# Row and layer norms by halves: mean spread and taken off apart, factors spread without a diagonal, other orders at four joints

## The chip, the cores and the metric

One core of a Trainium2 chip. The time is microseconds of one execution on the device; the median of several runs counts. TensorE (PE) does the matrix products into PSUM, VectorE (DVE) and ScalarE (ACT) the elementwise work, GpSimd (POOL) a few additions, SyncE (SP) issues the loads of the weights.

## The reference, cut to what matters

A transformer block and two hybrid layers over 512 tokens of 1024 channels, all in float32. The first block (with 16 meta tokens beside the 512):

```
h  = h + rms_norm(mix @ w_out, ln_post_mix)       # mix: two attentions, sliding and forgetting
hn = rms_norm(h, ln_pre_ffn)
ff = (silu(hn @ gate) * (hn @ up)) @ w_down
h  = h + rms_norm(ff, ln_post_ffn)
```

Each of the two layers that follow:

```
u    = x * (1 + scale) + shift                     # scale, shift, gate from c, by one matrix
proj = u @ w_in                                    # convolution, short convolution, latent attention, gates
m    = g_a * y_a + g_b * y_b + g_c * y_c
x    = layer_norm(alpha * x + gate * (m @ w_o), ln_g, ln_b)
```

rms_norm divides by sqrt(mean(x^2) + 1e-6) over a token's 1024 channels; layer_norm takes off the mean first and divides by sqrt(var + 1e-5).

## The kernel before, in words

**Layout.** Activations lie transposed: 128 partitions are 128 channels, 8 tiles (KD) hold the 1024 channels, and the free axis is the 512 tokens, in some places in two halves c = 0, 1 of 256 (HC). A norm therefore sums over partitions and over the 8 tiles.

**Weights.** 134 slots of 1 MB (128 x 2048) stream through three buffers. SP loads slot g when slot g - 3 is used up (slot_done). ACT copies the slot to `w_hi` in a rounded format (`slot_hi`, L1330), and DVE subtracts to get `w_lo` (`slot_lo`, L1887); both can go by quarters (`part`). A product is three matmuls, hi x hi, hi x lo, lo x hi (`mm3`, L631 to L633), and so each moving operand has a high and a low half too (`Xh` by ACT, `Xl` by DVE, `x_rest` L2196).

**Order.** Each engine has one queue, written out by hand in program order. Semaphores join them: a product waits for `x_lo`, a square by ACT for the tile's read by DVE and for the last use of its buffer (there are two, `sq`), an addition to `acc` for its square.

**A norm.** ACT squares, DVE or POOL add the squares into `acc`, PE sums over partitions with a matmul against a column of ones, tokens on the partitions (`token_sums` L672, `down_sums` L1059, `block_sums` L1089). ACT takes the root, DVE the reciprocal `ri`, one value per token. To bring it back along the free axis, DVE multiplies the identity by `ri` (four blocks of 128 x 128, or two for a half: L1938, L2228, L2538), and PE multiplies a matrix of ones with that diagonal (`spread` L687, `down_spread` L1073, `half_spread` L1121): each partition of a PSUM bank then holds the factor of each token.

**The joints.** These are the places that the change touches.
- Start: norm 0 of the first block.
- First border: the last two slots of w_out (slots 11 and 12, tiles n = 0 to 7 read by DVE at L2100), the post-mix norm, the pre-FFN input, then the first two gate/up slots, S_GU and S_GU + 1 (`two_slots` L974). Ahead and between PE runs filler, `keep_busy` (L635), matmuls with no use of their result. DVE splits S_GU behind tile 2 and S_GU + 1 behind tile 5; ACT copies the latter behind square 4.
- Second border: the last w_down slot by halves (`down_slot` L1022), the post-FFN norm of half 0 while half 1 is multiplied, `down_x` (L2231: multiply, add to h), the two ACT copies of the next input (L1597), `x_rest`, and the first two slots of layer 0, whose products wait for x_lo tile by tile (L1142 to L1163). `second_half` (L2214) reads half 1's tiles; its tiles 2 to 7 count `late_y`, of which the first layer's products want four (L1141).
- Third border: the same between layer 0 and layer 1, with a layer norm. `half_mean` (L2541) makes delta (the mean), its diagonal, and the variance from the mean of squares; `half_root` the factor's diagonal; `half_spread` spreads both into one bank, and `half_x` (L2559) subtracts the mean and then multiplies, tile by tile. The sums of half 0 stand among the products of half 1, tile 0 (`SUM_STEPS`, L1304), those of half 1 at step 3 of the next layer (L1145).
- Tail: the same behind layer 1, where no products follow; ACT applies gain and offset and SP stores.

## Time and profile before

| | us |
|---|---|
| median of 3 runs (lowest, highest) | 1720.53 (1719.82, 1721.81) |
| profiled execution, its own time | 1722.89 |
| its span, first to last instruction | 1720.9 |
| PE busy | 1692.8 (98%) |
| DVE, ACT, POOL busy | 1074.5, 726.1, 155.0 |
| PE waiting for `Xl` of a product | 6.2 |

The mean granted clock of PE is 0.992 of full speed. The span counts from the first to the last instruction; the execution's own time has some 2 us around it. In the timelines each row has start, duration, engine, line of the kernel, operation, output <- inputs, shape, count, and in brackets the idle time of the engine just before it with what ended it. The ends of matmuls are modelled, and matmuls overlap: the spacing of starts is the better measure of their cost.

### The profile page before, as it was taken

Reading aid. Unit: us, or ns where it says so; the run is one execution under the profiler, and the core shown is the slowest. Engines: PE = TensorE matmul, PEld = TensorE weight load, DVE = VectorE, ACT = ScalarE, POOL = GpSimd, SP = SyncE. Lnnn points to the kernel's source line nnn. Section 1 sums busy time; section 2 is a strip of 40 time slices with the busy share of each in tenths; the row PEclk is TensorE's granted clock in tenths of the full one; section 3 lists DMA queues with packets and bytes.
Section 4 is the critical chain, followed back from the end, with each engine's and each line's share of the span. In section 5 each row is a group of like instructions: output and inputs, shape, how many; then the busy total and the mean of one; then the engine's idle time right before and its main releaser. Section 6 shows DMA issues by size and latency. Waiting matters only on the chain.

```text
span 1720.9 us, 21479 instructions
## 1 busy us (share of the span) xinstructions
PE 1692.8 (98%) x8592; PEld 1404.2 (82%) x8592; DVE 1074.5 (62%) x1811; ACT 726.1 (42%) x1155; POOL 155.0 (9%) x144
## 2 busy tenths in 40 slices
PE   8999999999999999999999999999999999999997
PEld 8877777888888888888888888889888888888886
DVE  7455556866665437735869665667654769666465
ACT  4436563322222237576423222536566433232533
POOL 2100000000000000111100000021211100000012
PEclk9999999999999999999999999999999999999998
DMA  4321012555554321321222222221322122222221
GB/s 177 129 98 50 26 50 86 190 198 194 192 193 168 111 93 57 117 79 74 74 89 93 95 93 97 96 98 50 123 98 75 53 95 98 98 98 98 82 90 50
DMA packets 31138, 177.49 MB, mean 103 GB/s; under 512 B 3677, under 2 KB 5869, under 8 KB 13886
## 3 DMA queue, kind: packets, MB, share of 16 engines
q1 hardware_dynamic: 22048, 144.71, 23.3%
q0 software_dynamic: 8608, 31.21, 5.1%
q8 instruction: 68, 1.11, 0.3%
q10 hardware_dynamic: 382, 0.19, 0.0%
q14 instruction: 32, 0.26, 0.0%
HBM read 171.28 MB, written 4.78 MB: 102 GB/s over the span
## 4 chain that ended last, share of the span: by engine, by line
PE 81%; DVE 2%; issue 1%; DMA 0%; ACT 0%; DVEq 0%; ACTq 0%
PE ps L631 26%; PE ps L632 25%; PE ps L633 25%; PE ps L1247 1%; PE ps L1235 1%; DVE h L1872 1%; PE ps L1091 1%; PE ps L669 0%; DMA w_raw<-in_w 0%; DVE w_lo L1872 0%; PE ps L1224 0%; ACT w_hi L1320 0%; PE ps L1126 0%; DVE acc L1872 0%; DVE tmp L1879 0%
## 5 line engine op out<-in xcount | busy, mean ns | idle before, releaser
L631 PE MATMUL ps<-Xh,w_hi 128*128 128x512 f32 (+2 forms) x1760 | 666.2, 379 | 8.1 <-DVE Xl L1872 6.2
L633 PE MATMUL ps<-Xh,w_lo 128*128 128x512 f32 (+2 forms) x1760 | 655.1, 372 | 0.0
L632 PE MATMUL ps<-Xl,w_hi 128*128 128x512 f32 (+2 forms) x1760 | 655.0, 372 | 0.0
L1872 DVE TENSOR_TENSOR w_lo<-w_raw,w_hi 128x2048 fp32r<-128x2048 f32 (+1 forms) x161 | 312.2, 1941 | 252.8 <-ACT w_hi L1320 252.5
L631 PEld LDWEIGHTS ps<-Xh,w_hi 128*128 128x128 f32 x1760 | 331.2, 188 | 72.9 <-issue 11.4
L1320 ACT ACTIVATE w_hi<-w_raw 128x2048 fp32r<-128x2048 f32 (+1 forms) x158 | 260.5, 1652 | 293.0 <-DMA w_raw<-in_w 270.3
L632 PEld LDWEIGHTS ps<-Xl,w_hi 128*128 128x128 f32 x1760 | 331.3, 188 | 58.7 <-issue 2.6
L633 PEld LDWEIGHTS ps<-Xh,w_lo 128*128 128x128 f32 x1760 | 331.0, 188 | 58.3
L1879 DVE SCALAR_TENSOR_TENSOR cacc<-ain,vec,cacc 128x512 f32<-128x512 f32 x240 | 166.4, 765 | 0.0
L1320 ACT ACTIVATE gt<-ps 128x512 f32<-128x512 f32 x48 | 28.6, 597 | 200.6 <-PE ps L633 200.5
L631 PE MATMUL ps<-act_h,w_hi 128*128 128x512 f32 (+1 forms) x192 | 71.5, 372 | 0.6 <-DVE act_l L1872 0.6
L632 PE MATMUL ps<-act_l,w_hi 128*128 128x512 f32 (+1 forms) x192 | 71.3, 371 | 0.0
L633 PE MATMUL ps<-act_h,w_lo 128*128 128x512 f32 (+1 forms) x192 | 71.3, 371 | 0.0
L1320 ACT ACTIVATE Pc<-ps,nmax 128x128 f32<-128x128 f32 (+1 forms) x64 | 33.9, 529 | 79.3 <-DVE nmax L2344 79.1
L1320 ACT ACT_TABLE_LOAD x46 | 59.0, 1283 | 3.8 <-issue 3.0
L2145 DVE CUSTOM_DVE_ANT_0 ada_prod<-ada_w,cact 128x1024 f32<-128x1024 f32 x44 | 53.8, 1223 | 0.1
L583 POOL DMA_DIRECT2D ada_w<-in_w_ada x48 | 25.5, 531 | 276.3 <-DVE ada_sum L2145 276.3
L631 PEld LDWEIGHTS ps<-act_h,w_hi 128*128 128x128 f32 x192 | 36.2, 188 | 7.2 <-DVE w_lo L1872 1.0
L633 PEld LDWEIGHTS ps<-act_h,w_lo 128*128 128x128 f32 x192 | 36.1, 188 | 6.3
L632 PEld LDWEIGHTS ps<-act_l,w_hi 128*128 128x128 f32 x192 | 36.2, 188 | 6.2
L607 POOL TENSOR_TENSOR Ql<-Q,Qh 128x512 fp32r<-128x512 f32 x16 | 20.8, 1303 | 218.9 <-ACT Kh L1320 218.9
L1872 DVE TENSOR_TENSOR tmp<-ps,R 128x512 f32<-128x512 f32 x22 | 15.2, 690 | 34.3 <-PE ps L633 33.2
(322 smaller groups left out, 2186.2 us busy)
## 6 DMA issues: line engine op xcount, KB each, us to landing
w_raw<-in_w SPq DMA_DIRECT2D x134, 1024.0 KB, 4.8
ada_w<-in_w_ada POOLq DMA_DIRECT2D x48, 512.0 KB, 4.6
bias_scratch<-brow POOLq DMA_DIRECT2D x2, 1312.0 KB, 5.9
h<-in_xT SPq DMA_DIRECT2D x4, 512.0 KB, 5.9
out<-h SPq DMA_DIRECT2D x8, 256.0 KB, 2.1
bias<-bias_scratch POOLq DMA_DIRECT2D x1, 1024.0 KB, 8.8
bias<-bias_scratch POOLq DMA_DIRECT2D x1, 512.0 KB, 4.6
cact<-in_c POOLq DMA_DIRECT2D x1, 512.0 KB, 6.3
```

The source lines that it names most:

```text
L583: pool.dma_start(ada_w[:, t % 2, :], a["w_ada"][t, :, :]).then_inc(adaw_in[t % 2], 16)
L607: nc.gpsimd.tensor_tensor(Ql[:, :], Q[:, hd, :], Qh[:, :], ALU.subtract)
L631: nc.tensor.matmul(o_, whi, xhi, start=start, stop=False)
L632: nc.tensor.matmul(o_, whi, xlo, start=False, stop=False)
L633: return nc.tensor.matmul(o_, wlo, xhi, start=False, stop=stop)
L1091: last = nc.tensor.matmul(bank(b, 1, c0=t), src[:, HC * c + t * P:HC * c + (t + 1) * P], ones[:, 0:1], start=start and t == 0, stop=stop a ...
L1235: last = nc.tensor.transpose(bank(2 + b, P, c0=P * k), Pc[:, P * (tri(b) + k):P * (tri(b) + k + 1)], ident[:, :])
L1247: last = nc.tensor.matmul(bank(B_O, P, DH * e, DH * (e + 1), c0=P * b), Vc[:, k, DH * (hd - 1 + e):DH * (hd + e)], PTc[e][:, P * (tri(b) + ...
L1320: return nc.scalar.activation(o_, i_, f, **kw)
L1872: return nc.vector.tensor_tensor(o_, a_, b_, op)
L1879: return nc.vector.scalar_tensor_tensor(o_, a_, s_, b_, op0, op1)
L2145: nc.vector.tensor_tensor_reduce(prod, ada_w[:, par, :], cact[:, :], 1.0, 0.0, ALU.mult, ALU.add, ada_sum[:, par:par + 1]).then_inc(ada_do ...
```

## The change

- All spreads: no diagonal is made. The stationary operand of the spread is the column `ri[:, t]` itself, repeated over 128 columns, and the moving one is the identity. `diag_done` becomes `factor_done`, set by the reciprocal.
- First border: `keep_busy(2)` ahead of the sums goes. DVE splits S_GU behind tile 4 and S_GU + 1 behind the whole loop, ACT copies S_GU + 1 behind square 6, and DVE adds squares 5 and 6 between the reads of tiles 6 and 7.
- Second border: `x_rest` is taken out of `down_x` as `down_rest` and comes one or two steps later; quarters 0 and 1 of the slot are copied and split earlier; `down_x` of half 0 is mixed with the reads and additions of half 1; the spread of half 0 goes before tile 4 of the last slot, the sums and spread of half 1 before steps 5 and 6.
- Third border and tail: mean and factor are spread by matmuls of their own, into banks of their own; `half_sub` subtracts the mean as soon as it is spread, while variance, root and reciprocal are made, and `half_x` only multiplies. The sums have another order (mean first, then acc, then the two squares). In the tail four of the six sums of half 1 stand among the last tile's products.

```diff
-SUM_STEPS = (1, 2, 4, 5, 6, 7)
+SUM_ORDER = (0, 1, 2, 5, 3, 4)
...
             def spread(n, b):
-                pe.wait_ge(diag_done, n)
+                pe.wait_ge(factor_done, n)
                 for t in range(NB):
-                    last = nc.tensor.matmul(bank(b, P, c0=P * t), ones[:, :], tmp[:, 1, t * P:(t + 1) * P],
+                    last = nc.tensor.matmul(bank(b, P, c0=P * t), ri[:, t:t + 1].to_broadcast([P, P]), ident[:, :],
                                             start=True, stop=True)
...
-            keep_busy(2, bank(B_O), T)
             token_sums(1, 2 * KD - 1, (KD - 1,), B_ST)
...
                                 if j == 3:
                                     down_sums(0, 0)
-                                if j == 5:
+                                if j == 4:
                                     down_spread(0, 0)
...
-                    block_sums(var_bank, acc, c, False, True).then_inc(sum_full, 1)
+                    block_sums(var_bank, acc, c, True)
...
+            def block_spread(b, col, c):
+                for t in range(2):
+                    last = nc.tensor.matmul(bank(b, P, c0=P * t), col[:, 2 * c + t:2 * c + t + 1].to_broadcast([P, P]),
+                                            ident[:, :], start=True, stop=True)
+                return last
+            def mean_spread(L, c):
+                pe.wait_ge(delta_done, 2 * L + c + 1)
+                block_spread(spread_banks(L, c)[0], delta, c).then_inc(m_spread, 1)
+            def factor_spread(L, c):
+                pe.wait_ge(factor_done, SPREADS1 + 2 * L + c + 1)
+                block_spread(spread_banks(L, c)[1], ri, c).then_inc(r_spread, 1)
...
-                        if c == 0 and k == 3:
+                        if c == 0 and k == 4 and L:
+                            mean_spread(L - 1, 1)
+                        if c == 0 and k == (3 if L else 5):
...
-                        if c == 0 and k == KD - 3:
+                        if c == 0 and k == (5 if L else 6):
...
-                            if c == 1 and j == 0 and k in SUM_STEPS:
-                                half_sum(L, 0, SUM_STEPS.index(k))
-                            if c == 1 and j == 1 and k == 4:
-                                half_spread(L, 0)
+                            if c == 1 and j == 0:
+                                if k == 4:
+                                    mean_spread(L, 0)
+                                if k < len(SUM_ORDER):
+                                    half_sum(L, 0, SUM_ORDER[k])
+                            if c == 1 and j == 1 and k == 1:
+                                factor_spread(L, 0)
+                            if L + 1 == LAYERS and c == 1 and j == 1 and k >= 4:
+                                half_sum(L, 1, (0, 5, 1, 3)[k - 4])
...
                 if L + 1 == LAYERS:
-                    half_sums(L, 1)
-                    half_spread(L, 1)
+                    half_sum(L, 1, 2)
+                    half_sum(L, 1, 4)
+                    mean_spread(L, 1)
+                    factor_spread(L, 1)
...
                     if n == 2:
                         slot_hi(S_GU)
-                    if n == 4:
+                    if n == 6:
                         slot_hi(S_GU + 1)
...
-                    if n > 1:
+                    if n == 4:
+                        slot_lo(S_GU)
+                    if 1 < n < 6:
                         add_y_square(n - 1)
-                    if n == 2:
-                        slot_lo(S_GU)
-                    if n == 5:
-                        slot_lo(S_GU + 1)
+                    if n == 6:
+                        add_y_square(5)
+                        add_y_square(6)
+            slot_lo(S_GU + 1)
...
             down_add(1, 1)
+            slot_lo(SLOTS1 + 1, 0)
             down_roots(0)
             second_half(3)
-            slot_lo(SLOTS1 + 1, 0)
+            slot_lo(SLOTS1 + 1, 1)
             down_x(0, 0)
+            down_x(1, 0)
+            second_half(4)
+            down_rest(0, 0)
             down_add(2, 1)
-            second_half(4)
+            down_x(2, 0)
+            down_rest(1, 0)
             second_half(5)
...
+                def half_sub(j, c):
+                    cs = slice(HC * c, HC * (c + 1))
+                    if j == 0:
+                        ve.wait_ge(m_spread, 2 * L + c + 1)
+                        ve.wait_ge(sq_ready, SQ1 + SQUARES2 * (L + 1) - 2 + 2 * c)
+                    centred[j, c] = own.mark(tt(h[:, j, cs], h[:, j, cs], bank(spread_banks(L, c)[0], HC), ALU.subtract))
...
+                half_delta(0)
+                for j in range(3):
+                    half_sub(j, 0)
+                half_var(0)
+                half_sub(3, 0)
                 half_root(0)
                 if L + 1 == LAYERS:
+                    for j in range(4, KD):
+                        half_sub(j, 0)
+                    half_tile(KD - 2, 1)
+                    for j in range(KD):
+                        half_x(j, 0)
+                    half_tile(KD - 1, 1)
+                    half_delta(1)
+                    half_sub(0, 1)
+                    half_var(1)
+                    half_sub(1, 1)
+                    half_root(1)
+                    half_sub(2, 1)
+                    for j in range(KD):
+                        half_x(j, 1)
+                        if j + 3 < KD:
+                            half_sub(j + 3, 1)
```

## Rows read from the trace of the kernel before

**Rows 1.** Whom PE waited for: us in total, times, longest.

```profile
PE ps L631 <- DVE Xl L1872: 6.2, 7, 1.6
```

**Rows 2.** Timeline of PE, first border: start, us, instruction, idle before.

```profile
274.30 1.88 PE L639 MATMUL ps<-mask,ident 128*128 128x512 f32 x4
278.84 1.86 PE L678 MATMUL ps<-ones,acc 128*128 128x1 f32 x8 [2.67 <-DVE acc L1872]
...
284.12 1.81 PE L691 MATMUL ps<-tmp,ones 128*128 128x128 f32 x8
...
289.63 0.47 PE L631 MATMUL ps<-Xh,w_hi 128*128 128x512 f32 x1 [1.12 <-DVE Xl L1879]
```

**Rows 3.** Timeline of DVE, first border.

```profile
274.10 2.29 DVE L1872 TENSOR_TENSOR w_lo<-w_raw,w_hi 128x2048 fp32r<-128x2048 f32 x1 [0.83 <-ACT w_hi L1320]
...
278.11 0.68 DVE L1872 TENSOR_TENSOR acc<-acc,sq 128x512 f32<-128x512 f32 x1
...
285.97 0.75 DVE L1879 SCALAR_TENSOR_TENSOR tmp<-y,vec,ps 128x512 f32<-128x512 f32 x1 [2.13 <-PE ps L691]
```

**Rows 4.** Timeline of ACT, first border.

```profile
272.09 1.90 ACT L1320 ACTIVATE w_hi<-w_raw 128x2048 fp32r<-128x2048 f32 x1
...
277.07 0.63 ACT L1320 ACTIVATE sq<-y 128x512 f32<-128x512 f32 x1 [2.56 <-issue]
```

**Rows 5.** Windows: length, busy PE, PEld, DVE, ACT, POOL, then granted clock, DMA, GB/s.

```profile
278.50:279.00 0.50, 0.16 (x1) 0.16 (x1) 0.29 (x1) 0.40 (x1) 0.00 (x0) 0.86 0.13 49
285.50:286.00 0.50, 0.50 (x4) 0.46 (x4) 0.03 (x1) 0.00 (x0) 0.00 (x0) 0.82 0.00 0
1705.50:1706.00 0.50, 0.50 (x5) 0.50 (x4) 0.47 (x3) 0.42 (x1) 0.00 (x0) 0.63 0.34 115
```

**Rows 6.** Timeline of PE, third norm, among products.

```profile
308.80 0.95 PE L678 MATMUL ps<-ones,acc 128*128 128x1 f32 x8
...
311.77 1.05 PE L691 MATMUL ps<-tmp,ones 128*128 128x128 f32 x8
```

**Rows 7.** Timeline of PE, second border.

```profile
654.27 0.28 PE L631 MATMUL ps<-act_h,w_hi 128*128 128x256 f32 x1
...
654.63 0.28 PE L631 MATMUL ps<-act_h,w_hi 128*128 128x256 f32 x1
...
656.32 0.35 PE L631 MATMUL ps<-Xh,w_hi 128*128 128x256 f32 x1 [1.17 <-DVE Xl L1872]
...
662.62 0.39 PE L631 MATMUL ps<-Xh,w_hi 128*128 128x256 f32 x1 [1.59 <-DVE Xl L1872]
```

**Rows 8.** Timeline of DVE, second border.

```profile
653.04 0.48 DVE L1879 SCALAR_TENSOR_TENSOR tmp<-y,vec,ps 128x256 f32<-128x256 f32 x1
653.56 0.43 DVE L1872 TENSOR_TENSOR h<-h,tmp 128x256 f32<-128x256 f32 x1
653.90 0.42 DVE L1872 TENSOR_TENSOR acc<-acc,sq 128x256 f32<-128x256 f32 x1
```

**Rows 9.** Timeline of PE, third border.

```profile
1178.90 0.28 PE L631 MATMUL ps<-Xh,w_hi 128*128 128x256 f32 x1
...
1180.78 0.35 PE L631 MATMUL ps<-Xh,w_hi 128*128 128x256 f32 x1 [1.36 <-DVE Xl L1872]
...
1182.81 0.39 PE L631 MATMUL ps<-Xh,w_hi 128*128 128x256 f32 x1 [0.37 <-DVE Xl L1872]
```

**Rows 10.** Timeline of PE, tail.

```profile
1703.86 0.58 PE L1091 MATMUL ps<-ones,R 128*128 128x1 f32 x4 [0.82 <-DVE h L1879]
...
1709.20 2.08 PE L1126 MATMUL ps<-tmp,ones 128*128 128x128 f32 x8 [1.70 <-DVE tmp L1876]
```

**Rows 11.** Timelines of DVE and of ACT, tail.

```profile
1711.31 6.39 DVE L1872 TENSOR_TENSOR h<-h,ps 128x256 f32<-128x256 f32 x16 [0.60 <-PE ps L1126]
...
1717.73 0.60 ACT L1320 ACTIVATE h<-h,vec 128x256 f32<-128x256 f32 x1 [0.19 <-DVE h L1872]
```

**Rows 12.** Timeline of PE, start.

```profile
15.40 2.08 PE L691 MATMUL ps<-tmp,ones 128*128 128x128 f32 x8 [0.42 <-DVE tmp L1876]
```

More of the change, by code:

```diff
@@ L385, in program, with sum_banks, spread_banks @@
         B_O, B_ST = 6, 7
+        def sum_banks(L, c):
+            return (3, 4) if c == 0 else (0, 1) if L + 1 < LAYERS else (2, 5)
+        def spread_banks(L, c):
+            return (B_O, B_ST) if c == 0 else (0, 1) if L + 1 < LAYERS else (3, 4)
         LAT_BANK = (2, 3, 4, 5, 0, 6)
@@ L1073, in down_spread @@
             def down_spread(c, b):
-                pe.wait_ge(diag_done, 4 + c)
+                pe.wait_ge(factor_done, 4 + c)
                 for t in range(2):
-                    last = nc.tensor.matmul(bank(b, P, c0=P * t), ones[:, :], tmp[:, 1, HC * c + t * P:HC * c + (t + 1) * P],
-                                            start=True, stop=True)
+                    last = nc.tensor.matmul(bank(b, P, c0=P * t), ri[:, 2 * c + t:2 * c + t + 1].to_broadcast([P, P]),
+                                            ident[:, :], start=True, stop=True)
                 last.then_inc(r_spread, 1)
@@ L1609, in _ @@
             tf.add(KD - 1)
+            for part in range(2):
+                slot_hi(SLOTS1 + 1, part)
             for j in range(3):
@@ L1612, in _ @@
             down_root(0, 0)
-            slot_hi(SLOTS1 + 1, 0)
             down_square(3, 1)
             down_x(0, 0)
+            down_x(1, 0)
             down_square(4, 1)
-            slot_hi(SLOTS1 + 1, 1)
-            down_x(1, 0)
-            for j in range(5, KD):
-                down_square(j, 1)
+            down_x(2, 0)
+            down_square(5, 1)
+            down_x(3, 0)
             slot_hi(SLOTS1 + 1, 2)
-            down_x(2, 0)
-            down_x(3, 0)
+            down_square(6, 1)
+            down_x(4, 0)
+            down_x(5, 0)
+            down_square(7, 1)
             slot_hi(SLOTS1 + 1, 3)
-            down_x(4, 0)
             down_root(1, 1)
-            for j in range(5, KD):
+            for j in range(6, KD):
                 down_x(j, 0)
@@ L1935, in token_roots @@
                 ve.wait_ge(rt_done, norm + 1)
-                own.link(nc.vector.reciprocal(ri[:, :], rs[:, :]))
-                for t in range(NB):
-                    last = ts(tmp[:, 1, t * P:(t + 1) * P], ident[:, :], ri[:, t:t + 1], None, ALU.mult)
-                last.then_inc(diag_done, 1)
+                nc.vector.reciprocal(ri[:, :], rs[:, :]).then_inc(factor_done, 1)
             for j in range(1, KD):
@@ L2225, in down_roots @@
                 ve.wait_ge(rt_done, 4 + c)
-                own.link(nc.vector.reciprocal(ri[:, two], rs[:, two]))
-                for t in range(2 * c, 2 * c + 2):
-                    last = ts(tmp[:, 1, t * P:(t + 1) * P], ident[:, :], ri[:, t:t + 1], None, ALU.mult)
-                last.then_inc(diag_done, 1)
+                nc.vector.reciprocal(ri[:, two], rs[:, two]).then_inc(factor_done, 1)
             def down_x(j, c):
@@ L2595, in _ @@
-                for j in range(KD):
-                    half_x(j, 1)
-                if L + 1 == LAYERS:
+                half_delta(0)
[3 more added lines that the diff above has]
+                half_sub(3, 0)
+                half_root(0)
+                if L + 1 == LAYERS:
+                    for j in range(4, KD):
[14 more added lines that the diff above has]
+                            half_sub(j + 3, 1)
@@ L2598, in _ @@
                     ve.wait_ge(ln_out, 2 * KD)
                     return
-                x_rest(2 * KD * (L + 2) - 1, KD - 1, slice(HC, T))
+                half_sub(4, 0)
+                second_slot(0)
+                half_x(0, 0)
+                half_sub(5, 0)
+                half_x(1, 0)
+                second_slot(1)
+                half_rest(0, 0)
+                half_sub(6, 0)
+                half_x(2, 0)
+                half_tile(KD - 2, 1)
+                half_rest(1, 0)
+                half_sub(7, 0)
@@ new lines, in _ @@
+                half_x(3, 0)
+                half_tile(KD - 1, 1)
+                half_rest(2, 0)
+                second_slot(2)
+                half_x(4, 0)
+                half_rest(3, 0)
+                half_x(5, 0)
+                second_slot(3)
+                half_rest(4, 0)
+                half_x(6, 0)
+                half_rest(5, 0)
+                half_x(7, 0)
+                half_delta(1)
+                half_rest(6, 0)
+                half_var(1)
+                half_rest(7, 0)
@@ L2601, in _ @@
+                half_root(1)
+                half_sub(0, 1)
+                half_sub(1, 1)
+                half_x(0, 1)
+                half_sub(2, 1)
+                for j in range(1, KD):
+                    half_x(j, 1)
+                    if j + 2 < KD:
+                        half_sub(j + 2, 1)
+                    half_rest(j - 1, 1)
+                half_rest(KD - 1, 1)
                 assert own.n == OWN2, own.n
```

133 lines of the change are left out of this document (61 added, 72 removed).

## The prediction

> **What bounds the kernel now.** The page comes first: TensorE (PE) is busy for 98% of the span at a granted clock of 0.992, and every other engine has room, so time can only come out of places where PE stands still or does filler. The list of whom PE waited for shows where they are: the largest entry is products that wait for the low half of their moving operand, 6.2 us in seven waits [rows 1]. The timeline puts five of these at the second and third border; beside them stand the first border, where small sums, filler and a spread run one after the other [rows 2], and the tail, where PE has no product left and VectorE (DVE) and ScalarE (ACT) finish alone [rows 10, 11]. So the reader should see four joints between stretches of dense products, and read the change from them. The reference point is the profiled execution, 1722.89 us (span 1720.9 and 1.99 around it); it is 2.36 above the median of the runs, and I take that off at the end.
>
> **Start (norm 0).** The four scaled identity blocks go, and the spread reads the reciprocal itself. PE waited 0.42 for them [rows 12]; the filler ahead of the spread ends just where that wait began, so no more than this comes free, and the split pieces that DVE does meanwhile are shorter than the spread. Bounds 0 and 0.42; value 0.4.
>
> **First border.** Before: products are issued until 274.30, then 1.88 of filler, 2.67 of idle until the last addition to acc, sums, filler, spread; the first multiply stands at 285.97 and the first product at 289.63 [rows 2, 3]. The addition was late because DVE took up the 2.29 us split of the second gate/up slot at 274.10, ahead of the tiles 6 and 7, which it should have read [rows 3]. The change moves this split behind the loop, the first slot's split two tiles back, and ACT's half of the second slot (1.90) behind square 6.
> New order, step by step from the same end of products. A tile takes twelve products, 2.72 us, so tile 6 is complete near 271.8; reading, squaring and adding it are about 0.68 + 0.63 + 0.68 [rows 3, 4], so acc is whole near 273.8, before the products end. Hence the acc sums run at once, and only tile 7 is left: read from about 274.5 to 275.1, squared until 275.8. ACT's slot copy, begun near 273.05, ends at 274.95, by its 1.90 [rows 4], and just doesn't delay that square; were it 0.5 us later, so would be the border. Sums of square 7 at the full clock, 0.8 to 0.95 [rows 6], end near 276.7. The slot's split on DVE (2.2, from 275.1) now stands ahead of the reciprocal, which comes at 277.4; that is as late as ACT's root and PE's one remaining filler allow. Spread 1.05 [rows 6]: first multiply near 278.74 instead of 285.97, and the 3.66 us from there to the first product stay. Gain 7.2. The two filler products that are dropped are worth nothing by themselves; what they guarded is the clock, below.
>
> **Clock at this border.** By the means of half-microsecond windows the granted clock fell to 0.5 (1.2 GHz) near 278.85, after PE had stood still since 276.2, and came back near 285.7, after some 6.8 us of sums, filler and spread; sums of 8 instructions took 1.86 there, 0.95 at the full level [rows 2, 5, 6]. In the tail it fell near 1705.65, with PE issuing one-column sums since 1703.86 [rows 5, 10]. It did not fall over the stops of 1.17 to 1.59 at the second border [rows 7]. In the new order the longest stop before the products is about 0.5, then sums, 0.94 of filler and the spread, and three fillers afterwards; I take the full clock. If it falls all the same, sums, filler and spread from 275.9 on cost 0.85 + 0.94 + 1.0 more: gain 4.4 instead of 7.2.
> The Trainium skill speaks against the change here: TensorE: Matmul & The Clock Gate, section Why this matters for your kernels, asks to leave no long stops between bursts, since they bring the half rate back, and its Part 1 says that the chip's watch runs free of the kernel's start, so that the same order may fall in one run and not in another. By that rule, removing filler is a risk, and the border would give 4.4. This trace agrees with the fall at 278.85 and at 1705.65 and shows shorter stops without one.
>
> **Third norm inside the products.** Its spread at 311.77 waited for nothing; the chain from its end to the next tile is unchanged. 0.
>
> **Second border.** Three products take 0.36 us, a step of twelve 1.44 [rows 7]. Products would have gone on at 654.99; steps 0 and 2 started at 656.32 and 662.62, so that 1.33 was lost ahead of the first and 6.30 - 2.88 = 3.42 in the two that follow, in all 4.75. New queue of DVE, from 651.96, with 0.34 for a half tile's addition, 0.86 for a multiply and its addition [rows 8], about 0.60 for a quarter split (a quarter of 2.29 and an instruction's fixed part): second_half 3, quarter 1, down_x 0 and 1, second_half 4 (3.0), rest 0 (behind ACT's two copies of block 0, 655.05), add 2, down_x 2, rest 1, second_half 5 (2.2): 657.3. That last one matters, since the next layer's first product waits for the fourth late_y, which second_half 5 gives: it stood before 655 and now stands behind rest 1. So the first product comes later than before, near 657.45: a stop of 2.46. From there the low halves are ready at 656.9, 658.8, 660.7, 662.8, 664.4, each before its step (657.45 + 1.44 each); the sums, moved two steps later, find their squares; about 0.14 is lost at the last step. Gain 4.75 - 2.6 = 2.2. Bounds: 4.7 with no stop left, -0.5 if DVE is a further 2.7 late.
>
> **Third border.** PE lost 1180.78 - 1179.26 = 1.52 and 1182.81 - 1180.78 - 1.44 = 0.59 [rows 9]. The mean's sums move one or two steps earlier, and its spread and subtraction run under tile 0's products while the variance's sums and root are made; behind the factor only the multiply is left. By the same counting the delta comes 0.7 earlier, the first multiply near 1176.9, the first low half near 1178.5, ahead of the last product. ACT's quarter copy ahead of half_x 1 leaves low half 1 at 1180.05, within 0.1 of its step. The added spread costs PE 0.1. Gain 2.0; bounds 0.5 (the first stop merely halved, the second kept) and 2.1. The second half's sums at step 3 find their inputs 1.5 us early.
>
> **Tail.** Before: sums from 1703.86, spread at 1709.20, sixteen operations from 1711.31, last ACT operation 1717.73 to 1718.33 [rows 10, 11], then 2.57 of output. New: four sums go among the last tile's products, about 0.45 each (0.58 for a lone one, [rows 10]), so these end at 1704.7, not 1703.0. Then tile 7's half, 0.5; its sums and the delta, 0.8; mean spread to the first subtraction, 0.75: 1706.8. Variance, ACT's root, reciprocal and two subtractions take 1.1; the factor's spread is half of the 2.08 that eight took [rows 10]: 1708.95. Thirteen operations then remain, not sixteen, and a multiply no longer waits for its own subtraction: 0.34 apart [rows 8] instead of 6.39 / 16 = 0.40; ACT follows at 0.5 for the last two: end at 1714.3 against 1718.33. Gain 4.0; bounds 2.5 (spreads at the half clock throughout, 0.40 kept) and 4.6.
>
> **Sum.** 0.4 + 7.2 + 2.2 + 2.0 + 4.0 = 15.8: 1707.1 for a profiled execution, 1704.7 for the median. Between the joints PE runs without stops that hang on an absolute time, so I expect nothing to be given back.
>
> **Not in the trace: a stationary operand that repeats one column.** 32 matmuls, 64 loads, take `ri` or `delta` broadcast over 128 columns where `ones` or a diagonal stood; the number of loads stays. The nearest row is the spread with a dense operand, eight loads and passes in 1.05 [rows 6], and I take that. Below it a gain of 0.05 each at most is left; above, nothing in the trace bounds it, and it is a rival.
> The Trainium skill prices it, on the page TensorE: Matmul & The Clock Gate, section LDWEIGHTS, by the number of columns alone, with 107 ns for 128 columns at its rate; an estimate by that page adds nothing to the sum. No run here shows it.
>
> **Rivals.**
> - The clock falls at the first border: +2.8, 1707.5. For: two falls at such places. Against: the new stops are shorter than those it outlasted.
> - The second and third border give nothing (+4.2, 1708.9): a DVE queue of the same length, or ACT's two copies per block, keep the low halves as late as before. For: the first product of the second border is later by my own count. Against: at the third border nothing but the split of the chain is needed.
> - On the other side, one mechanism: the broadcast loads are slow. All 64 stand at joints where PE or DVE waits for them. 15.8 / 64 = 0.25 us more for each eats the gain, 0.30 makes the kernel slower by over 0.2%, 0.5 gives 1721. For: no such load in the trace. Against: the loads are many columns of one value, no more bytes than before.
>
> **How the numbers follow.** A measurement tells 0.2% (3.4 us) from no change. Forecast 0.6 (own range 1702.5 to 1706.5), clock 0.18, borders 0.13, loads 0.05 (slower), and 0.04 for several terms failing at once, most of it within the bound. The range 1702.5 to 1710 takes in the first three cases nearly whole. Faster 0.92 (the first three and a part of the last), same 0.03, slower 0.05.
>
> **What would show it.** First border: no 2.29 us split between the tile reads, acc sums right behind the last product, first multiply some 4.3 after it, clock 1.0. Second: one stop of about 2.4 before the first product and none behind steps 0 to 2. Third: no stop over 0.2. Tail: four sum groups among the last products, thirteen operations behind the last spread. A spread over 1.3 us at the full clock, or stops that stay at the second and third border, would make it wrong.

## The result and the profile after

| | before | after |
|---|---|---|
| median of the timed runs, us (lowest, highest, runs) | 1721.17 (1719.82, 1722.25, 4) | 1710.26 (1710.12, 1711.40, 4) |
| ratio after / before, 95% interval | | 0.9938 [0.9922, 0.9954] |
| profiled execution, us | 1722.89 | 1710.12 |
| its span, us | 1720.9 | 1708.3 |

The kernel is 10.9 us faster by the medians, and 12.8 in the profiled executions (12.6 of it in the span). The forecast was 15.8 and 1704.7, its range ended at 1710.0: the direction is right, the time lies 0.26 outside. Ratios and their intervals, here and below, are of undisturbed executions; two slow ones stand outside them (2119 us of the kernel before, 3373 us of one further down).

The changed kernel's page, its line of the engines, and then its list of whom PE waited for (total us, times, longest) answer to [rows 1]: of the seven waits for `Xl`, 6.2 us, one of 1.1 and two of 0.3 together are left; a wait for `y` (the first product of the second border) and one for `act_l` (w_down) have come up.

```profile
PE 1687.0 (99%) x8588; PEld 1401.2 (82%) x8588; DVE 1065.2 (62%) x1779; ACT 723.3 (42%) x1155; POOL 154.8 (9%) x144
```

```profile
PE ps L640 <- DVE y L1905: 2.1, 1, 2.1
PE ps L640 <- DVE act_l L1905: 1.7, 1, 1.7
PE ps L1130 <- DVE ri L2593: 1.2, 1, 1.2
PE ps L640 <- DVE Xl L1912: 1.1, 1, 1.1
```

The view that settles where the time went is none of the page's: both traces hold the same 7080 matmuls of `mm3` (called products from here on, as in the prediction's counts), so the start of each can be subtracted from the start of the same product before. Where this lead grows or shrinks, the change gains or loses. The entries are read to within 0.03.

| place | forecast | lead gained in the profiled pair |
|---|---|---|
| start | 0.4 | 0.53 |
| first border | 7.2 | 7.06 |
| third norm | 0 | 0.0 |
| w_down stage | 0 | -1.06 |
| second border, and 20 us behind it | 2.2 | 2.28, then -0.57 |
| third border | 2.0 | 0.84 |
| tail | 4.0 | 3.53 |
| sum | 15.8 | 12.6 |

**First border**, PE of the changed kernel, against [rows 2]: sums right behind the products, one stop of 0.71, spread 1.05 where it was 1.81. The first product stands at 282.08 where it stood at 289.63.

```profile
273.81 0.95 PE L687 MATMUL ps<-ones,acc 128*128 128x1 f32 x8
275.47 1.05 PE L692 MATMUL ps<-ones,sq 128*128 128x1 f32 x8 [0.71 <-ACT sq L1344]
276.38 1.10 PE L648 MATMUL ps<-mask,ident 128*128 128x512 f32 x2
277.32 1.05 PE L700 MATMUL ps<-ident,ri 128*128 128x128 f32 x8
278.21 2.74 PE L648 MATMUL ps<-mask,ident 128*128 128x512 f32 x6
...
282.08 0.47 PE L640 MATMUL ps<-Xh,w_hi 128*128 128x512 f32 x1 [1.13 <-DVE Xl L1912]
```

**w_down stage**, the changed kernel's chain of work that ended last (start, us, what), then PE's row: a weight slot took 7.38 us from issue to landing (median 4.8 in this stage), and the products behind it stood still for 1.67.

```profile
589.96 7.38 DMA w_raw<-in_w
597.35 0.03 ACTq L1352
597.37 0.04 issue
597.42 1.93 ACT w_hi L1344
...
599.44 2.29 DVE w_lo L1905
601.73 0.61 DVE act_l L1905
```

```profile
602.48 0.47 PE L640 MATMUL ps<-act_h,w_hi 128*128 128x512 f32 x1 [1.67 <-DVE act_l L1905]
```

**Third border**, windows of the changed kernel (length, busy PE, PEld, DVE, ACT, POOL, granted clock, DMA, GB/s). PE has no wait left, but the clock is at 0.5 for some 3.4 us, behind 24 one-column sums issued in one go from 1175.39 to 1177.98 (24 as the profile counts: each of the kernel's twelve float32 matmuls shows as two). In the profiled execution of before, none of the windows from 1165 to 1194 was under 1.00; the second fence has its window behind the sums.

```profile
1178.00:1179.50 1.50, 1.50 (x14) 1.50 (x14) 0.99 (x4) 1.12 (x3) 0.00 (x0) 0.92 0.00 0
1179.50:1181.00 1.50, 1.50 (x9) 1.50 (x9) 0.27 (x1) 0.00 (x0) 0.00 (x0) 0.50 0.00 0
1181.00:1182.50 1.50, 1.50 (x9) 1.50 (x9) 0.48 (x2) 0.00 (x0) 0.00 (x0) 0.50 0.00 0
1182.50:1184.00 1.50, 1.50 (x14) 1.50 (x14) 0.46 (x2) 0.00 (x1) 0.00 (x0) 0.94 0.00 0
```

```profile
1185.00:1190.00 5.00, 5.00 (x45) 4.88 (x44) 2.16 (x10) 1.61 (x4) 0.00 (x0) 1.00 0.00 0
```

**Second border and tail**: PE, then DVE's last group, against [rows 7, 10, 11]. One stop of 2.15 replaces three; a stop of 0.30 follows 25 us later, for a weight slot's low half; in the tail four groups of sums stand among the products (the first at 1692.39), and thirteen operations remain behind the last spread.

```profile
650.80 0.35 PE L640 MATMUL ps<-Xh,w_hi 128*128 128x256 f32 x1 [2.15 <-DVE y L1905]
...
676.30 0.50 PE L640 MATMUL ps<-Xh,w_hi 128*128 128x512 f32 x1 [0.30 <-DVE w_lo L1905]
...
1692.39 0.50 PE L1099 MATMUL ps<-ones,R 128*128 128x1 f32 x4
...
1696.34 0.61 PE L1099 MATMUL ps<-ones,h 128*128 128x1 f32 x4 [0.58 <-DVE h L1912]
1696.81 0.59 PE L1099 MATMUL ps<-ones,sq 128*128 128x1 f32 x4
...
1699.11 1.22 PE L1130 MATMUL ps<-ident,ri 128*128 128x128 f32 x4 [1.17 <-DVE ri L2593]
```

```profile
1700.38 4.40 DVE L1905 TENSOR_TENSOR h<-h,ps 128x256 f32<-128x256 f32 x13 [1.00 <-PE ps L1130]
```

### The profile page after: what moved, and what is told of

Read it like the earlier page. It is cut to its first block, busy times and chain, and to the rows that moved or that the text cites. A ratio compares the mean times of both kernels' runs of the same rounds, so it can differ in the third digit from the quotient of the medians.

```text
span 1708.3 us, 21445 instructions
## 1 busy us (share of the span) xinstructions
PE 1687.0 (99%) x8588; PEld 1401.2 (82%) x8588; DVE 1065.2 (62%) x1779; ACT 723.3 (42%) x1155; POOL 154.8 (9%) x144
## 4 chain that ended last, share of the span: by engine, by line
PE 96%; DVE 2%; DMA 1%; ACT 1%; issue 0%; ACTq 0%; DVEq 0%
PE ps L640 29%; PE ps L642 29%; PE ps L641 28%; PE ps L1264 1%; PE ps L1252 1%; PE ps L875 1%; PE ps L905 1%; PE ps L838 1%; DVE h L1905 1%; PE ps L1099 1%; PE ps L897 1%; PE ps L678 1%; PE ps L870 0%; PE ps L836 0%; DMA w_raw<-in_w 0%; PE ps L849 0%
```

## The experiments

Theory: the forecast's mechanisms hold, and what is missing went to (a) falls of TensorE's clock at joints that I had taken as safe, (b) the weight slot in w_down, (c) an order in the tail that costs instead of giving, and (d) a reference point that was no typical execution. Main rival: the missing 3 us belong to one accidental execution. Ratios are to the kernel before on the same chip; a difference of two ratios whose intervals overlap is no proof by itself, and then the products of the profiled executions are what is read. Leads are again those of single products in the profiled executions, against the changed kernel's first profile.

### Both kernels once more

The changed kernel, no edit:

> The changed kernel once more, unchanged. Theory A: its two unforeseen losses belong to the order of its instructions. Then the stop of 1.67 us of TensorE near 602 (a w_down product behind a weight slot whose transfer took 6.15 instead of 3.5 us, begun 0.3 us after a block of instructions was fetched by DMA) and the fall of the clock to 0.5 near 1179 (3.4 us long, right behind the 24 one-column sums) come again within 0.3 us of their places, and the span is 1708.3 within 1. Rival: both are accidents of one execution; then at least one is missing, the span is 1.3 to 3.2 us shorter, and the median of the timed runs is below 1709.

Ratio 0.9935 [0.9921, 0.9949], median 1710.87, profiled span 1709.9. Half of each came: the missing time is there again in sum, partly at other places. The stop in w_down came again (1.98, a transfer of 6.45 us by its packets, begun 0.25 behind a fetch of instructions), with a small one (0.23) ahead of it. The fall near 1179 did not: that border came out 1.53 better. Instead the clock fell at the second border, 1.49 worse there, and at the first, 0.45 worse. PE's row and, in the second fence, the window of the fall in this execution:

```profile
602.99 0.47 PE L640 MATMUL ps<-act_h,w_hi 128*128 128x512 f32 x1 [1.98 <-DVE act_l L1905]
```

```profile
652.50:655.50 3.00, 3.00 (x16) 3.00 (x16) 2.97 (x9) 2.85 (x6) 0.00 (x0) 0.50 0.27 112
```

The kernel before, no edit:

> The kernel before once more, unchanged, for its clock. Theory: whether the clock falls at a border varies between executions of the same kernel, so this one has other falls than the first (278.86 for 6.83 us only): at the first border half as long or none, or a new one at the second or third border; and its span differs from 1720.9 by 0.5 to 3 us, by the places where the clock fell and by the transfer in the w_down stage that the fetch of a block of instructions delays. Rival: the falls belong to the kernel; then there is one fall, at 278.9 within 0.5, and the span is 1720.9 within 0.5.

One execution, 1721.72, span 1719.7. The fall at the first border lasted half as long (the sums took 1.05 there, not 1.86 as in [rows 2]), there was one at the third border that the first profile lacked, right behind the old order's own 24 sums (1183.59 to 1186.18), and no slow transfer in w_down. So the old order falls at the third border too, in some executions. The window of this fall:

```profile
1186.50:1189.50 3.00, 3.00 (x16) 3.00 (x16) 2.90 (x11) 1.78 (x4) 0.00 (x0) 0.50 0.00 0
```

From start to the first border's end the changed kernel's lead over this execution is 6.20, against 7.55 over the first one.

### The first border alone

The old order of this border comes back (the first slot's split and the squares too); the new spread stays.

```
-                    if n == 6:
+                    if n == 4:
                         slot_hi(S_GU + 1)
...
+                    if n == 5:
+                        slot_lo(S_GU + 1)
...
-            slot_lo(S_GU + 1)
...
+            keep_busy(2, bank(B_O), T)
             token_sums(1, 2 * KD - 1, (KD - 1,), B_ST)
```

> The changed kernel with the first border's order as before: split of the second gate/up slot ahead of the reads of tiles 6 and 7, its copy on ScalarE behind square 4, two filler products ahead of the sums. Theory: this border alone gives 7.0 of the 12.6 us, so the kernel takes 7.0 (6.5 to 7.5) us more than the changed one, and the clock falls near 278 again. Rival: part of what is gained there is given back at later places that hang on other clocks (the weight slots of w_down), then it is 5 to 6.3 more.

Ratio 0.9962 [0.9949, 0.9975], median 1715.11: 4.2 above the changed kernel on the same chip, under both expectations. By products the undone border cost 5.4; the wait for acc is back (277.50, stop 2.67), but the clock's fall was half as long as in [rows 2, 5]. So of the 7.06 in the profiled pair some 1.6 was the longer fall of that one execution of before, and the changed order falls there too, in other executions. PE's rows of this execution:

```profile
277.50 1.05 PE L687 MATMUL ps<-ones,acc 128*128 128x1 f32 x8 [2.67 <-DVE acc L1906]
278.41 1.03 PE L692 MATMUL ps<-ones,sq 128*128 128x1 f32 x8
```

### Sums at the third border in two groups

```
-                        if c == 0 and k == (3 if L else 5):
-                            if L:
-                                for i in SUM_ORDER:
-                                    half_sum(L - 1, 1, i)
+                        if c == 0 and k in (2, 3) and L:
+                            for i in SUM_ORDER[3 * (k - 2):3 * (k - 1)]:
+                                half_sum(L - 1, 1, i)
...
```

> The changed kernel with the 24 one-column sums of the second half at the third border put in two groups, the mean's 12 at step 2 and the variance's 12 at step 3, with twelve products between them, instead of all at step 3. Theory: the clock falls at 1179 because 2.6 us of one-column sums stand together; split, it stays full there, and the border gains 1.2 to 1.6 us. Rival 1: the fall does not hang on their standing together, and comes again; change within 0.3. Rival 2: the mean's sums wait for their inputs at step 2 and open a stop; 0.3 to 1 slower there.

Ratio 0.9924 [0.9911, 0.9937], median 1708.48, 2.4 below the changed kernel on the same chip, with overlapping intervals. No fall and no stop at this border, which came out 1.55 better than in the first profile. One execution without a fall proves little, since the unchanged order has such executions; the test by the opposite follows.

### The first half's sums in one go

```
-                                if k == 4:
+                                if k == 6:
                                     mean_spread(L, 0)
-                                if k < len(SUM_ORDER):
-                                    half_sum(L, 0, SUM_ORDER[k])
+                                if k == 4:
+                                    for i in SUM_ORDER:
+                                        half_sum(L, 0, i)
```

> The changed kernel with the first half's 24 one-column sums, which stand in six groups among as many steps of the last tiles of each layer, all at one step, and the mean's spread two steps later; the third border stays as changed. Theory: standing together is what lets the clock fall, so that it now falls also near 1166 to 1172 (end of layer 0) or near 1686 to 1692 (end of layer 1), in at least one of the two, 1.4 to 1.6 us each, and the median is 1 to 3 us above the changed kernel's. Rival: together or apart is no matter; no fall at either place, and the same time within 0.5.

Ratio 0.9953 [0.9941, 0.9966], against 0.9935 for the changed kernel: 0.18%, 3.1 us, the upper end of what the theory gave, though the intervals overlap. The clock fell in the middle of the layer's end, where it had never fallen in the eleven other profiles of changed orders; PE's rows, then the window of this execution:

```profile
1161.34 0.50 PE L1099 MATMUL ps<-ones,R 128*128 128x1 f32 x4
1161.70 1.03 PE L1099 MATMUL ps<-ones,h 128*128 128x1 f32 x8
1162.59 0.59 PE L1099 MATMUL ps<-ones,acc 128*128 128x1 f32 x4
1163.04 1.29 PE L1099 MATMUL ps<-ones,sq 128*128 128x1 f32 x8
```

```profile
1163.70:1167.00 3.30, 3.30 (x17) 3.30 (x17) 0.24 (x1) 0.00 (x0) 0.00 (x0) 0.50 0.00 0
```

The layer's end came out 2.4 worse, 0.53 of it a stop for the factor (the edit put the mean's spread two steps later). At the end of layer 1, the other place named, it did not fall. Its third border, with the sums in one go as before, happened to stay at the full clock.

### The second border: each bank's own wait, or filler

```
-                if L == 0:
-                    pe.wait_ge(late_y, 4)
...
+                            if L == 0 and c == 0 and k == 0:
+                                pe.wait_ge(late_y, i + 1)
...
             down_rest(0, 0)
-            down_add(2, 1)
-            down_x(2, 0)
-            down_rest(1, 0)
             second_half(5)
+            down_x(2, 0)
+            down_rest(1, 0)
+            down_add(2, 1)
             down_add(3, 1)
```

> The changed kernel with another start of the products at the second border: each of the first four products waits only for its own PSUM bank to be read, and VectorE takes second_half 5 two operations earlier. The first product came at 650.80 behind a stop of 2.15. Theory: the stop ends 1.5 to 1.8 earlier (stop 0.4 to 0.7); the low halves of steps 3 to 6 are late then, and 0.3 to 1.6 of it is kept behind step 7, likeliest 0.8; with the shorter stop the clock does not fall near 652, as it did in three of five executions of such orders (1.5 us each). Rival: the low halves on VectorE are the bound from step 2 on, and the same end of the border comes out, within 0.2, with other stops; the clock then falls or not as before.

Ratio 0.9928 [0.9916, 0.9941], median 1709.50. The first product came 1.85 earlier, and all of it was lost again by step 7 (the lead over the changed kernel is 1.68 ahead of the border, 1.52 behind it): the rival is right, the low halves on DVE and ACT are the bound. No fall at this border. The stops of this execution:

```profile
647.27 0.35 PE L640 MATMUL ps<-Xh,w_hi 128*128 128x256 f32 x1 [0.30 <-issue]
651.03 0.39 PE L640 MATMUL ps<-Xh,w_hi 128*128 128x256 f32 x1 [0.60 <-DVE Xl L1905]
652.88 0.39 PE L640 MATMUL ps<-Xh,w_hi 128*128 128x256 f32 x1 [0.17 <-DVE Xl L1905]
655.00 0.38 PE L640 MATMUL ps<-Xh,w_hi 128*128 128x256 f32 x1 [0.43 <-DVE Xl L1905]
```

The other way, filler in the stop:

```
                 if L == 0:
+                    pe.wait_ge(bank_read[1], FILL1[1])
+                    keep_busy(8, bank(1), T)
                     pe.wait_ge(late_y, 4)
```

> The changed kernel with eight filler products (512 columns, 0.234 us each) in the stop of 2.15 us ahead of the second border's first product. Theory: the clock falls at this border in some executions because TensorE stands still there; with the filler it stays full, the first product comes at the same time within 0.1, and the median is 0.5 to 1.5 us shorter than the changed kernel's. Rival 1: the fall comes of something else (it began 1.2 us after the stop had ended); it is seen at 650 to 657 all the same. Rival 2: the filler delays the products by 0.2 to 0.5.

Ratio 0.9954 [0.9941, 0.9966], median 1712.64: slower than the changed kernel, by my own mistake. A filler of 512 columns takes 0.88 here, not 0.234 (a float32 product shows as two matmuls, x16 for eight), so they held the products back by 4.16:

```profile
648.89 7.03 PE L648 MATMUL ps<-mask,ident 128*128 128x512 f32 x16
```

The clock did stay full at this border; the right number of fillers, two, is in the last group below.

### The tail's sums behind the last tile

```
-                            if L + 1 == LAYERS and c == 1 and j == 1 and k >= 4:
-                                half_sum(L, 1, (0, 5, 1, 3)[k - 4])
...
-                    half_sum(L, 1, 2)
-                    half_sum(L, 1, 4)
+                    for i in (0, 5, 1, 3, 2, 4):
+                        half_sum(L, 1, i)
```

> The changed kernel with the second half's four groups of sums behind the last tile's products again, not among them; the rest of the tail stays as changed. Among the products they cost 1.26 us of TensorE time by the trace; behind them they stand on the path to the end, about 1.3 at the full clock and 2.6 at 1.2 GHz. Theory: their place is worth 0 to 0.5 if the clock is full until they end, 1 to 1.5 if it falls among them (it fell at 1696.9 to 1698.1 in two executions), so the kernel is 0.2 to 1.5 us slower. Rival: the last tile's addition on VectorE and the root hide them, and nothing changes (within 0.2), so the whole gain of the tail is in the split of mean and factor.

Ratio 0.9934 [0.9921, 0.9948], median 1709.65: not to be told from the changed kernel by the timed runs, as the rival has it. By products the tail of this execution is 0.83 shorter, where five executions with the changed tail agree with the first within 0.02 (in one more, the second run of the changed kernel, the clock fell earlier in the tail and it took 1.2 longer); in the three kernels further down with the sums behind, it is 0.59, 1.36 and 0.85 shorter. So the theory is wrong in sign. The rows show why: less the lead that this execution had before, the products end 1.77 earlier, and the sums now fill the 0.58 in which PE had waited for tile 7.

```profile
1693.37 0.50 PE L1099 MATMUL ps<-ones,R 128*128 128x1 f32 x4
...
1695.08 0.58 PE L1099 MATMUL ps<-ones,h 128*128 128x1 f32 x4
1695.52 0.58 PE L1099 MATMUL ps<-ones,sq 128*128 128x1 f32 x4
1695.97 0.69 PE L1130 MATMUL ps<-ident,rsum 128*128 128x128 f32 x4
1697.83 1.23 PE L1130 MATMUL ps<-ident,ri 128*128 128x128 f32 x4 [1.17 <-DVE ri L2591]
```

### More warm-up at the start

```
-            warm_up(8, 4)
+            warm_up(28, 4)
```

> The changed kernel with 28 instead of 8 warm-up products (128 columns, 0.127 us each) ahead of the first norm's sums, in the 2.77 us that TensorE waits there. It does two things. First, theory: the clock, at 0.5 from 11.9 to 18.7 in the changed kernel, stays full; the sums take 0.95 instead of 1.87, the spread 1.05 instead of 1.92, and the first product comes 1.5 to 1.8 us earlier, all of it kept. Rival: the clock falls there whatever TensorE does, or the first product hangs on the weights' low half; gain under 0.3. Second, all later blocks of TensorE's instructions are fetched 20 products earlier (4.7 us in the w_down stage). Theory: the stop of 1.67 near 602 comes of the fetch that lies on the transfer of a weight slot, so it goes (another 1.0 to 1.7). Rival: the transfer is late for another reason, and the stop stays at 1.4 to 1.9. Both theories together: 2.5 to 3.4 us less than the changed kernel.

Ratio 0.9936 [0.9923, 0.9948], median 1711.38: nothing gained. The twenty added products took 4.6 us, not 2.5 (the same miscount), so the sums came 1.57 late, at 13.88; they and the spread then ran at the full clock (0.95 and 1.16). The first product, at 18.81, came 0.40 earlier than in the first profile, but that is no gain: in the ten profiles with the changed kernel's own warm-up it stood between 17.93 and 19.50, early where the clock's fall at the start lasted 3.4 us and late where it lasted 6.8. In w_down the stop near 602 was gone; a stop of 0.45 stood at 558.88 instead, behind a transfer of 4.79 us.

### Together

The edits of the third border (two groups), the tail (sums behind) and the second border (own waits); then the same with two fillers in the stop instead of the own waits; then the first with `warm_up(18, 4)`.

> Three edits on the changed kernel: the 24 sums at the third border in two groups (as in e3), the tail's sums behind the last tile (as in e4), each bank's own wait at the second border (as in e5). Theory: TensorE's clock then falls at neither the second nor the third border (it fell near the first of these in 4 of 6 executions of the order with the 2.15 us stop, near the second in 6 of 7 with all 24 sums together; 1.5 us each), and the tail ends 0.8 earlier: 1707.3 (1706 to 1708.5) where the changed kernel takes 1710.5. Rival: the falls come at chance at any joint; then one is seen at the third border again, and the kernel is 0.8 to 1.5 better than the changed one, not 3.

> As the kernel with three edits, but at the second border the changed kernel's own wait for four banks stays, and two filler products (512 columns; such a filler takes 0.94 us, so 1.9 of the 2.15 us stop) stand in it. Theory: no fall near 652, the first product at the same place as in the changed kernel within 0.15, and 1707.2 (1706 to 1708.5). Rival: the clock falls there though TensorE is not idle.

> The kernel with three edits and ten more warm-up products in the 2.8 us that TensorE waits at the start: TensorE's blocks of instructions are fetched ten products (2.3 us) earlier in the w_down stage, so that the fetch that began 0.25 to 1.05 us ahead of the transfer near 591 now ends 1.4 us ahead of it. Theory: a fetch that begins up to 1.1 us ahead of a weight slot's transfer is what stretches it (in about half the cases, by 1.1 to 3), and what goes beyond 0.97 becomes a stop; so no transfer of the w_down stage takes over 4.3 us, no stop over 0.15 us stands between 535 and 645, and the kernel is 0 to 1.5 us, in the mean 0.9, better than the one with three edits. Rival: transfers are stretched at random; a stop of 0.2 to 2 is seen in the stage.

| kernel | ratio to before, 95% | median, us | profiled span, us |
|---|---|---|---|
| three edits | 0.9916 [0.9903, 0.9929] | 1706.79 | 1705.5 |
| filler in the stop | 0.9913 [0.9900, 0.9926] | 1706.38 | 1703.3 |
| three edits, warm start | 0.9911 [0.9898, 0.9923] | 1705.47 | 1705.2 |

The first two are 0.5 and 0.8 better than expected, the third within what was expected, and all beat the changed kernel: 0.9911 / 0.9935 is 0.24%, 4.1 us. None fell at the second or third border; a window of the first of them (the changed kernel had 0.50 here) and the two stops in w_down of the third:

```profile
1179.50:1181.00 1.50, 1.50 (x15) 1.50 (x14) 0.75 (x2) 0.00 (x0) 0.00 (x0) 1.00 0.00 0
```

```profile
568.49 0.47 PE L640 MATMUL ps<-act_h,w_hi 128*128 128x512 f32 x1 [1.48 <-DVE act_l L1902]
...
623.49 0.47 PE L640 MATMUL ps<-act_h,w_hi 128*128 128x512 f32 x1 [0.31 <-DVE act_l L1902]
```

In the third the expectation on w_down failed. The start gained 1.8 over the first profile and 0.5 over the best of the ten (sums at 12.31 at the full clock, spread 1.16), but fetches stood 0.80 and 0.96 ahead of two transfers again, which took 5.93 and 4.76. Ten more warm-up products, which the page counts as twenty matmuls, did not move the fetches by ten products' time; where they put them, I had no means to foresee.

### What the fourteen profiles show of the clock and of the slow transfers

| fall of the clock at | with | without |
|---|---|---|
| second border, stop of 2.15 empty | 4 of 7 executions | |
| second border, stop cut or filled | | 0 of 5 |
| third border, 24 sums in one go, changed orders | 6 of 8 | |
| third border, 12 and 12 | | 0 of 4 |
| third border, 24 sums in one go, old order | 1 of 2 | |
| first border, changed order | 7 of 11 | |

Each fall at the second or third border cost 1.5 (3.1 in two executions where it lasted twice as long), at the first 0.45 to 2.2. The counts are small: were the places chance, a split as clean as the first two rows would come in 7% of cases, as the third and fourth in 3%; what speaks most for the sums is the fall that came where the first half's were put together. Why the clock fell at the first border in seven of eleven executions, with stops of only 0.71 and 1.13 and with filler between, no run settles.

In w_down, by the packets' own times: of 25 transfers with a fetch of instructions begun 0.2 to 1.1 us ahead, 10 took 4.6 to 6.5 us. Of 114 others one took as long, with a fetch inside it (4.79); 99 had no fetch in or just ahead of them, and took 3.36 to 3.78. Every transfer over 4.47 became a stop of its length less 4.34 to 4.48: 0.59 from 5.07 in the first profile of before, 1.67 from 6.15 after. The Trainium skill has both halves of this, in DMA: Bandwidth & Descriptors, section Queues, rings and completion order (a DMA engine serves the queues that have work for it in turn, a packet at a time), and in Runtime: NRT & Kernel Launch, section Instruction fetch mechanics (code comes in 16 KiB blocks through a DMA queue of the engine's own, "mostly hidden"). The trace agrees with the blocks (a single packet of 16 KiB on the instruction queue beside the slow transfer); no run here shows the turns, and the ten cases speak against the "mostly hidden" only if the fetch is their cause. That it causes the delay is not shown: fifteen transfers with such a fetch were not as slow, no run took a fetch away, and moving it failed twice to clear the stage.

## Why the prediction was wrong

**What bounds the kernel, third norm**: right. All gains came from the joints; the spread with the repeated column took 1.05 for eight, so the rival of slow loads is gone. (One figure of that rival does not follow: 64 loads at 0.5 more each are 32 us and give some 1737, not 1721; nothing hung on it.)

**Start**: the diagonal's wait is gone, as forecast. The 0.53 of the pair lies above the bound of 0.42 and is no measure of it: the first product of the changed start varies by 1.6 between executions, with the clock's fall there.

**First border**: right as a mechanism and in the pair (7.06 for 7.2; the sums at 273.81, the multiply at 278.41 as worked out). Against other executions of the old order it is 5.4 to 5.5, and 4.2 by the medians: the fall in [rows 5], which I counted as before's own, is shorter in others, and the changed order falls as well. So the 7.2 was over-sized by 1.7 to 3.0 as a term for typical executions. "I take the full clock" failed in 7 of 11 executions, at 0.45 to 2.2 each, under the 2.8 of that rival; the stops before the products were 0.71 and 1.13, not "about 0.5" at the longest.

**Second border**: 2.28 for 2.2, one stop where forecast, for the reason forecast. But "nothing to be given back" failed here: DVE begins the split of the next layer's third weight slot 7.5 earlier than before (673.96), PE reaches its products 8.8 earlier; 0.57 is given back at 676.30, and a stop of 0.28 to 0.31 stands there in every profile of a changed order. The split before, then after:

```profile
681.48 2.29 DVE L1872 TENSOR_TENSOR w_lo<-w_raw,w_hi 128x2048 fp32r<-128x2048 f32 x1 [1.45 <-ACT w_hi L1320]
673.96 2.29 DVE L1905 TENSOR_TENSOR w_lo<-w_raw,w_hi 128x2048 fp32r<-128x2048 f32 x1 [1.45 <-ACT w_hi L1344]
```

And in 4 of 7 executions the stop of 2.15, which I had compared with the 1.17 to 1.59 of [rows 7], was followed by a fall of the clock: 1.5 more.

**Third border**: the queue is right: no stop is left, and in the two executions of these sums without a fall it gained 2.37 and 2.38. The size failed, 0.84, by the clock: I had weighed the fall only at the first border, though I had cited the rows in which one-column sums preceded one in the tail [rows 10]. In part that is the pair's luck: the profiled execution of before had no fall here and that of after had one, but the old order falls here too, and against its second execution, with a fall on both sides, the border gained 2.17. The same order falls in some executions and not in others. The Trainium skill's rule in TensorE: Matmul & The Clock Gate, Part 1, that the watch does not start with the kernel, agrees with this; no run here shows the watch itself.

**Tail**: 3.53 for 4.0. Thirteen operations, 0.34 apart, as forecast. The first of them began 0.5 later than worked out (1700.38; 1708.95 less the lead of 9.06 is 1699.89), which is the whole of what is missing. What failed besides is the edit's own idea: sums among the last products push these by 1.77 (1.7 forecast) and leave PE waiting 0.58 for tile 7, and behind them they cost less.

**w_down**: the step that failed outright. "Between the joints PE runs without stops that hang on an absolute time": the chain of waits of before had such a transfer in it, of 6.31 from issue to landing, and a stop of 0.59 at 576.33; I did not follow it. Such transfers cost 0.87 of lead in the profiled execution of before and 1.93 in that of after, hence the -1.06. The changed orders had fetches just ahead of two transfers of the stage in eleven of twelve profiles, before of one in both of its own. The transfer and the stop of before, from its chain of waits and from PE's row:

```profile
564.88 6.31 DMA w_raw<-in_w
...
576.33 0.47 PE L631 MATMUL ps<-act_h,w_hi 128*128 128x512 f32 x1 [0.59 <-DVE act_l L1872]
```

**Reference point**: I took 2.36 off for the profiled execution of before standing above the median. Over all runs the medians of before are 1721.17 to 1722.77, and the profiled execution of after stands 0.14 under its median. So the deduction was wrong by 2.5 of the 5.5 missed. Some 1.6 of it, as far as the other two executions of the old order at the first border show, is the longer fall there, which the 7.2 already takes out: it was taken off twice. The other 3.0 are the sum (15.8 against 12.6, and 0.17 less around the span): -1.06 w_down, -1.16 third border, -0.49 second with what it gave back, -0.47 tail; start and first border cancel.

## What to carry to other kernels

Take a joint's worth from several executions, not one: here the clock's falls between start and tail moved a profile by 0 to 5.3 us, and a difference of two single profiles holds both kernels' luck. When an order puts many one-column sums in one go, or leaves an empty stop of two microseconds, count a fall of the clock (1.5 us) with its chance, also where PE is busy by the page; sums in two groups, or two fillers in the stop, cost nothing here. Before sums are put among products to save time later, ask whether PE waits behind those products anyway.

## What the runs showed of the hardware that was not expected

The granted clock fell to the lower level while PE was busy without a stop: behind 24 one-column sums in 2.6 us in 6 of 8 executions of the changed orders, behind twelve, twelve products and twelve more in none of 4 (twelve float32 matmuls, which the profile counts as 24). A weight transfer of 1 MB that otherwise took 3.4 to 3.8 us took 4.6 to 6.45 in ten of 25 cases with a 16 KiB fetch of instructions begun just ahead of it. A float32 filler of 512 columns took 0.88 to 0.94 us, where one matmul of 512 columns of `mm3` takes 0.23, and a row counts it as two.
